# Fetching the first expert block before the routing is finished: a hybrid encoder step on one Trainium2 core

## The reference

```python
x = x + mix @ w_out                                   # the mixer, heads and pooling
h = rmsnorm(x, norm2_g)
pg_top, g = top_k(softmax(h @ w_rg + b_rg), 1)        # one of 4 groups
pv, pi = top_k(softmax((h @ w_re + b_re)[group g]), 2)  # two of its 4 experts
for e in range(16):                                   # D_MODEL 1024, D_EXPERT 512
    y = y + gates[:, e] * ((silu(h @ w_gate[e]) * (h @ w_up[e])) @ w_down[e])
out = rmsnorm(x + y, norm_f_g)
```

## Time and profile before

| what | value |
|---|---|
| median of 3 runs | 953.19 us (952.35 to 956.46) |
| profiled execution, its own time | 953.14 us |
| its span in the trace | 951.5 us |
| mixer stage, to the first instruction of block 1 | 547.29 us |
| blocks 1 to 15 | 547.29 to 904.15 us |
| last block's down product and the final norm | 904.15 to 951.5 us |

### The profile page before, as it was taken

The page is one execution under the profiler, slowest core; times in us unless marked ns, Lnnn a source line. Parts: engine busy times, 40 slices in busy tenths (PEclk is TensorE's granted clock), DMA queues, the critical chain, the costliest instruction groups (busy, mean ns, idle before and its releaser), DMA issues. The chain is left out here.

```text
span 951.5 us, 16708 instructions
## 1 busy us (share of the span) xinstructions
PE 885.8 (93%) x6335; PEld 753.2 (79%) x6335; DVE 435.8 (46%) x1169; ACT 145.6 (15%) x447; POOL 367.7 (39%) x572
## 2 busy tenths in 40 slices
PE   5989999999999999999986799999999999999960
PEld 3975969779596795968853399999999999999910
DVE  2245474737537365463656723434333333333254
ACT  2123122221312212121121000000000000000060
POOL 4050040300303012030120466777777777766512
PEclk9999999999999999999998799999999999999985
DMA  9931111030300202011065169999999999999874
GB/s 330 299 122 22 47 15 31 1 78 2 69 10 11 69 1 56 1 12 45 1 185 180 42 216 302 358 339 356 342 346 345 340 330 324 320 311 312 235 260 148
DMA packets 89973, 162.06 MB, mean 170 GB/s; under 512 B 48843, under 2 KB 58979, under 8 KB 81722
## 3 DMA queue, kind: packets, MB, share of 16 engines
q1 hardware_dynamic: 71210, 137.02, 41.2%
q0 software_dynamic: 17664, 24.23, 11.2%
q10 hardware_dynamic: 1040, 0.00, 0.1%
HBM read 138.78 MB, written 24.82 MB: 172 GB/s over the span
## 5 line engine op out<-in xcount | busy, mean ns | idle before, releaser
L1437 PE MATMUL bank<-wout,win 128*128 128x130 f32 (+3 forms) x2048 | 246.4, 282 | 3.1 <-DVE wout L1313 3.1
L1437 PEld LDWEIGHTS bank<-wout,win 128*128 128x128 f32 x2048 | 244.8, 191 | 3.2 <-DVE wout L1313 3.2
L1437 PE MATMUL bank<-hT,win 128*128 128x128 f32 (+1 forms) x1536 | 182.9, 279 | 0.0
L1437 PEld LDWEIGHTS bank<-hT,win 128*128 128x128 f32 x1536 | 178.6, 192 | 1.5 <-issue 1.2
L575 POOL DMA_INDIRECT z_d<-wout,win x75 | 119.3, 1590 | 27.9 <-issue 27.6
L1437 PE MATMUL bank<-win 128*128 128x130 f32 (+5 forms) x992 | 129.5, 290 | 0.0
L1437 PEld LDWEIGHTS bank<-win 128*128 128x128 f32 (+2 forms) x992 | 118.5, 188 | 8.9 <-issue 8.9
L1437 PE MATMUL bank<-win,hT 128*128 128x260 f32 (+3 forms) x512 | 119.7, 412 | 3.2 <-DMA win<-in_w_in 1.6
L1437 PE MATMUL bank<-wout,mixT 128*128 128x512 f32 (+1 forms) x384 | 118.5, 492 | 1.8 <-ACT mixT L815 1.7
L1437 PEld LDWEIGHTS bank<-win,hT 128*128 128x128 f32 (+1 forms) x512 | 76.1, 171 | 41.5 <-issue 32.5
L1437 PEld LDWEIGHTS bank<-wout,mixT 128*128 128x128 f32 (+1 forms) x384 | 51.4, 165 | 58.2 <-issue 55.5
(11 more groups left out here) (297 smaller groups left out, 821.4 us busy)
## 6 DMA issues: line engine op xcount, KB each, us to landing
win<-in_w_gate SPq DMA_DIRECT2D x32, 1024.0 KB, 6.2
win<-in_w_up SPq DMA_DIRECT2D x32, 1024.0 KB, 10.6
win<-in_w_down SPq DMA_DIRECT2D x32, 1024.0 KB, 9.6
win<-in_w_in SPq DMA_DIRECT2D x4, 2048.0 KB, 19.9
xbuf<-in_x_prompt SPq DMA_DIRECT2D x8, 512.0 KB, 3.9
wout<-in_w_out SPq DMA_DIRECT2D x1, 4096.0 KB, 15.2
z_d<-xbuf SPq DMA_DIRECT2D x32, 128.0 KB, 2.7
h_d<-xn SPq DMA_DIRECT2D x8, 512.0 KB, 2.8
```

What stands on the lines that cost most here:

```text
L1437: return nc.tensor.matmul(out, lhsT, rhs, start=first, stop=last)
```

## The change

The first block no longer waits for the complete list of expert 0. At i = LAST POOL writes the lists of the tiles up to 6, reads the first 150 entries of expert 0, and, after it has delivered the pooling mean, gathers those rows into a buffer of their own (`xg1`). An entry that is still empty brings row TOK, which now holds zeros (the plain store of a zero slice of `wr`). DVE turns and scales them (`first_turn`, `first_scale`) into `xgS` in the middle of the last tile's work. The rows of the last two tiles (`PICKED`, 7 and 8) are taken on PE instead: ACT copies the tile's rows from `xbuf` in another order (`xp`), DVE makes a matrix that holds the row's norm factor where the row's place in expert 0's list equals the column (`pick`), and `first_picks` on PE multiplies them, eight matmuls of 150 columns for each tile (16 instructions), added up in banks 2, 3 and 0. `first_rows` on DVE adds both parts into `xgT` in eight instructions.

Besides: expert 1 is fixed as well, as block 2 with 150 rows (so `SLOTS` has one more place of 150 and one fewer of 135); its list and its weights no longer wait for the table. `idraw` and `idt` have buffers of their own. The state's transposes on PE move ahead of `ranks(LAST)`. The copies and the stores of the state move from DVE and SP to ACT. POOL copies 256 rows of x_prompt into `h2_d` at i = 3, in place of values not yet written. `WARM` goes away. `first_turn` for block 1 and its five multiplies after the table go away, and `gather_turn(1)` comes after `products(1)`.

```diff
-    SLOTS = ((30, 1), (26, 6), (27, 3), (28, 2), (30, 2))
+    SLOTS = ((30, 1), (30, 1), (26, 6), (27, 2), (28, 2), (30, 2))
...
+        PICKED = (LAST - 1, LAST)
+        xp = [win[:, (15 + i) * D:(16 + i) * D].rearrange("p (k f) -> p k f", k=KD) for i in range(2)]
+        xg1 = win[:, 17 * D:17 * D + NP * PIECE].rearrange("p (a d) -> p a d", a=NP)
+        pick = [win[:, 19 * D + i * BLOCK:19 * D + (i + 1) * BLOCK].rearrange("p (a i) -> p a i", a=NP) for i in range(2)]
+        PICKB = ((2, 0, 3), (3, 3, 6), (0, 6, 8))
...
-        WARM = 14
...
-                sp.dma_start(rows[TOK, :].rearrange("(p n a) -> p n a", p=P, a=2), empty[:, 0:D // (2 * P), :]
-                             ).then_inc(S["ids_zeroed"], 16)
+                sp.dma_start(rows[TOK, :].rearrange("(p n) -> p n", p=P), wr[:, 0, NR:NR + D // P]).then_inc(S["ids_zeroed"], 16)
...
+                if t == PICKED[0]:
+                    after(sp, "h2_filled", 16)
...
-            after(sp, "table_ready", 1)
-            for c in range(NP):
-                sp.wait_ge(first[c], 16)
...
+            for half in range(2):
+                sp.wait_ge(*((gu_half, 2) if half == 0 else (gu_done, 8)))
+                load_gate_up(1, half)
+            for half in range(2):
+                sp.wait_ge(*((d0_used, 2) if half == 0 else (dn_done, 6)))
+                load_down(1, half)
+            after(sp, "table_ready", 1)
+            nblocks = sp.value_load(tabi[0:1, 2 * (NB + 1):2 * (NB + 1) + 1], min_val=NE, max_val=NB)
+            sooner = sp.value_load(tabi[0:1, 2 * (NB + 1) + 1:2 * (NB + 1) + 2], min_val=NE - 3, max_val=NB - 3)
+            with sp.Fori(3, nblocks + 1) as j:
...
+                if i == 3:
+                    early = [START[t] for t in PICKED]
+                    pool.dma_start(h2_d[min(early):max(early) + P, :], x_prompt[0, min(early):max(early) + P, :]
+                                   ).then_inc(S["h2_filled"], 16)
+                if i == LAST:
+                    scatter(i - 2)
+                    load_ids(0)
+                    pool.wait_ge(ids_in, 16)
+                    add_quarter(False)
...
+                    after(pool, "h2_stored", 16 * (LAST - 1))
+                    after(pool, "h2_filled", 16)
+                    after(pool, "u_done", NT)
+                    pool.wait_ge(carried, 1)
+                    gather_tokens(first, xg1)
+                elif 2 <= i:
...
             load_ids(0)
-            pool.wait_ge(ids_in, 16)
-            add_quarter()
+            pool.wait_ge(ids_in, 32)
+            g.tensor_copy(ents[0], idraw).then_inc(carried, 1)
             pool.wait_ge(carried, 2)
-            gather_tokens(first)
+            load_ids(CAP)
+            g.tensor_copy(ents[1], ents[0]).then_inc(rolled, 1)
+            pool.wait_ge(rolled, 1)
+            fetch_block(2, 2)
...
+                    a.activation(xp[t - PICKED[0]], xbuf[:, t % 4, :].rearrange("p (f k) -> p k f", k=KD), ACT.Copy
+                                 ).then_inc(xp_ready, 1)
...
+            after(act, "ulT_done", 1)
+            for n in range(2):
+                last = a.activation(uout[:, n, :], B[4 + n][0:HIST, :], ACT.Copy)
+            last.then_inc(S["ul_out"], 1)
+            after(act, "nT_done", 1)
+            a.activation(gt[:, :, :], B[6][0:H, 0:2 * P].rearrange("p (a b) -> p a b", a=2), ACT.Copy
+                         ).then_inc(S["nT_out"], 1)
+            after(act, "state_ready", NT)
+            for st, Co in ((Cp, C_prompt), (Cs, C_sample)):
+                act.dma_start(Co[0, 0].rearrange("h d v -> d h v"), st[:, :, 0:DH]).then_inc(S["stores"], 16)
...
+            def first_picks(t):
+                i, place = t - PICKED[0], rt[:, 80:81]
+                link(v.scalar_tensor_tensor(out=rt[:, 128 + i:129 + i], in0=oh[:, t, 2, 0:1], scalar=-NEAR, in1=place,
+                                            op0=ALU.mult, op1=ALU.add))
+                v.tensor_scalar(pick[i], place_of[:, :, :], rt[:, 128 + i:129 + i], sm[:, 11:12], ALU.is_equal, ALU.mult
+                                ).then_inc(pick_ready, 1)
+            def first_turn():
+                for c in range(NP):
+                    dve.wait_ge(first[c], 16)
+                    v.transpose(xgS[:, :, c, :], xg1[:, c, :].rearrange("p (i k) -> p k i", k=KD)).then_inc(xt_raw, 1)
+            def first_scale():
+                dve.wait_ge(xt_raw, NP)
+                v.tensor_tensor(xgS.rearrange("p k a i -> p k (a i)"), xgS.rearrange("p k a i -> p k (a i)"),
+                                wide(g2m[:, :], [P, KD, NP * 32]), ALU.mult).then_inc(base_scaled, 1)
+            def first_rows():
+                dve.wait_ge(base_scaled, 1)
+                after(dve, "out_done", NT)
+                for n, (b, k0, k1) in enumerate(PICKB):
+                    dve.wait_ge(picked, n + 1)
+                    for k in range(k0, k1):
+                        at = B[b][:, (k - k0) * BLOCK:(k - k0 + 1) * BLOCK].rearrange("p (a i) -> p a i", a=NP)
+                        v.scalar_tensor_tensor(out=xgT[:, k, :, 0:RP], in0=at, scalar=g2m[:, k:k + 1], in1=xgS[:, k, :, 0:RP],
+                                               op0=ALU.mult, op1=ALU.add).then_inc(gx_ready, 1)
...
                     h2_evac(LAST - 1)
+                    first_turn()
                     numerators(LAST)
                     partial_logits(LAST - 1)
                     head_out(LAST)
                     logits(LAST - 1)
                     routing(LAST - 1)
+                    first_scale()
                     residual(LAST)
...
+            first_rows()
...
-            def first_turn():
-                for c in range(NP):
-                    dve.wait_ge(first[c], 16)
-                    v.transpose(xgT[:, :, c, :], xg[:, c, :].rearrange("p (i k) -> p k i", k=KD)).then_inc(xt_raw, 1)
-                for c in range(NP):
-                    dve.wait_ge(xt_raw, c + 1)
-                    v.tensor_tensor(xgT[:, :, c, :], xgT[:, :, c, :], wide(g2m[:, :], [P, KD, 32]), ALU.mult).then_inc(gx_ready, 1)
...
+            products(1, SLOTS[0][0])
             gather_turn(1)
-            products(1, SLOTS[0][0])
...
+            def first_picks(t):
+                i = t - PICKED[0]
+                pe.wait_ge(xp_ready, i + 1)
+                pe.wait_ge(pick_ready, i + 1)
+                for b, k0, k1 in PICKB:
+                    for k in range(k0, k1):
+                        at = B[b][:, (k - k0) * BLOCK:(k - k0 + 1) * BLOCK].rearrange("p (a i) -> p a i", a=NP)
+                        last = mm(at, xp[i][:, k, :], pick[i], i == 0 and k == k0, i == 1 and k == k1 - 1)
+                    if i == 1:
+                        last.then_inc(picked, 1)
...
+                if i == NT + 1:
+                    first_picks(LAST - 1)
+                    state_transposes()
                 if 2 <= i:
                     ranks(i - 2)
+                if i == NT + 1:
+                    first_picks(LAST)
...
-            for _ in range(WARM):
-                mm(B[7][:, 0:512].rearrange("p (a b) -> p a b", a=4), ident[:, :],
-                   ident[:, :].unsqueeze(1).broadcast_to([P, 4, P]))
```

More of the change, by code:

```diff
@@ L562, in load_ids, with add_quarter @@
                                ).then_inc(ids_in, 16)
[L564 removed]
+            def add_quarter(keep=True):
                 g.tensor_scalar(idt, idraw[:, :, 0], qf[:, 0:1], None, ALU.add).then_inc(carried, 1)
[L567 removed]
+                if keep:
+                    g.tensor_copy(ents[0], idraw).then_inc(carried, 1)
+            after(pool, "hist_ready", 1)
+            after(pool, "ids_zeroed", 16 * 3)
+            for i in range(NT + 2):
+                if 1 <= i <= NT:
+                    causal(i - 1)
+                if i == 3:
[7 more added lines that the diff above has]
+                    add_quarter(False)
+                if i < NT:
+                    pool_mean(i)
+                if i == LAST:
+                    after(pool, "h2_stored", 16 * (LAST - 1))
[4 more added lines that the diff above has]
+                elif 2 <= i:
+                    scatter(i - 2)
             def stand(c):
@@ L1174, in _ @@
             link(v.tensor_scalar(ecap[:, :], iof[:, 0:NE], float(CAP), None, ALU.mult))
+            for a in range(NP):
+                v.tensor_scalar(place_of[:, a, :], iof[:, 0:RP], float(NP), a - NEAR, ALU.mult, ALU.add)
             p0 = 0
```

99 lines of the change are left out of this document (40 added, 59 removed).

## The result

The changed kernel takes **941.13 us** (median of 4 runs, 939.53 to 941.5), the kernel before, run beside it, 952.81 (4 runs). The ratio is 0.9868, 95% interval 0.9849 to 0.9887: faster by 1.3%. The forecast of 943.8 is a ratio of 943.8 / 953.19 = 0.9901, above that interval; the low end of the range, 940.5, is 0.9867. So sign and mechanism held, and the likeliest time was too slow by 2.7 us. The time fell where rival B stood (940.8, given a chance of 0.10); it also lies at the fast end of rival A's own range (941 to 946).

What follows compares the result with a forecast made beforehand. PE, busy 93% of the span, was taken to bound the kernel, with only block 1's start movable: start -11.8 us, larger block +2.4, so -9.4 and a forecast of 943.8 us, range 940.5 to 949.

Steps and rivals of the forecast that it cites:

- rival B: No clock dip and a quick clock: start 534.3, block 1 24.5, total 940.8 us; chance 0.10.
- rival A: The forecast as summed: 943.8 us, own range 941 to 946; chance 0.60.
- the routing: Expert stage: expert 1 gets 150 columns, still 16 blocks; one block costs 24.50 in place of 22.08 us, +2.4 us.
- POOL's early list: POOL before the last pooling mean: scatter, list load and offset take 8.0 of 10.0 idle us, costing nothing.
- the DVE part of the picks: Tile 7's pick matrix on DVE ahead of the last h2_evac: a scalar step and a compare, +0.45 us.
- the table's end: DVE's table, begun at 535.2, ends before 546.6; block 1's first silu product is due at 546.9: hidden by a hair.
- Block 2's rows: Gathered rows land at 552.2, are turned and scaled by 559.1 against a wanted 561.8: 2.7 us to spare.
- The copies on ACT: ACT's reordered copies into xp after each norm: 1.5 us taken, upper end 2.0, in 2.04 us idle; no cost.
- Block 1 itself: Block 1 on PE keeps its 26.3 us, clock dip included; ends 24.5 (no dip) and 28.
- step 6: PE between router sums and ranks: tile 7's picks and state transposes overfill the 4.75 us gap, +1.2 us (0.5 to 1.7).
- picks of tile 8: Sixteen PE instructions after the last places: 2.1 us at full clock to 4.1 at half, taken as 3.1.
- rival C: Clock stays low throughout: slower picks, block 1 28.0, output product loses 1.8 us; total 948.8 us; chance 0.15.

Runs made afterwards that it cites:

- The second run: The unchanged file of the changed kernel measured once more: 941.09 us, ratio 0.9858 against the kernel before.
- the one with the later turn: Changed kernel with first_turn moved on DVE behind routing(LAST-1) and first_scale put between the residual's halves: 940.65 us, ratio 0.9852.

## Why the prediction was right or wrong

**Right:** what bounds the kernel, and that block 1's start is the thing to move. PE's blocks have the lengths of the earlier trace rows, and the time follows the start. Also right, each by its row: the routing (16 blocks; +2.43 for +2.4, and +2.0 alone); POOL's early list (the pooling input finds POOL idle for 2.90 us at 470.97, forecast 2.0 to spare); the gathers, in before DVE's turn at 494.85, which waits for no DMA; `first_turn` at +1.33 for +1.6; the DVE part of the picks at +0.46 for +0.45; `first_scale` hidden; the table's end at 544.05 before the first silu product at 545.81. Block 2's rows are turned from 552.96 (forecast: landed at 552.2) and scaled by 556.99 against a wanted 558.75: 1.8 us to spare, forecast 2.7.

The copies on ACT took 2.04 us, at the forecast's upper end, not the 1.5 taken:

```profile
486.15 1.06 ACT L842 ACTIVATE xn<-xbuf 128x1024 f32<-128x1024 f32 x1 [3.98 <-DVE xbuf L1226]
...
487.77 2.04 ACT L845 ACTIVATE win<-xbuf 128x1024 f32<-128x1024 f32 x1
...
489.90 1.28 ACT L769 ACTIVATE dexp<-dexp,hmt 128x128 f32<-128x128 f32 x4
```

The same 1,024 columns take 1.06 us in order and 2.04 at a 32-byte step, and the decay matrix follows with no idle shown: the 2.04 us of the earlier trace rows were just enough. The Trainium skill ("SBUF — State Buffer", the note on cachelines) warns of this penalty without a price; the trace agrees and gives one, a factor of 1.9.

**Wrong, and the step that failed: "Block 1 itself ... I keep 26.3 us".** In the profiled execution, 941.5 us stand against a sum of 943.7. Block 1 measured 24.62, which is -1.7 us; its start is -1.4 us against the forecast; the kernel's end, +0.8, was not in the sum. The clock of 0.56 at block 1's start in the earlier trace rows was laid to no cause; it stood there after 3.15 us of idle, and the change leaves 1.15. The prediction named both gaps, left open whether the clock would be up, and kept the dip. The kernel before with 17 warm matmuls shows the cause: 0.58 us of idle, no dip. Rival B had both terms nearly right (start 534.3, block 1 24.5), with a chance of 0.10.

The second term of the same kind is PE in step 6 and the picks of tile 8. In the accounting of the last tile's chain:

| term, us | forecast | measured |
|---|---|---|
| slots of tile 6 later | 0 | +0.25 |
| `first_turn` | +1.6 | +1.33 |
| output product | 0 | +1.29 |
| `first_picks(7)` on DVE | +0.45 | +0.46 |
| PE up to the ranks | +1.2 | -0.4 |
| picks of tile 8 | 3.1 | 2.28 |

The first five add up to 2.9 us, as the ranks moved (528.66 - 525.75 = 2.91) where 3.25 were forecast; with the 0.8 of the picks that is nearly all of the 1.4 us by which block 1 starts earlier than the forecast 535.5.

Picks of tile 7 and transposes filled the gap of 4.75 us and no more. The picks did run at the low clock, 3.96 us for the 4.1 forecast:

```profile
524.00:527.00 3.00, 3.00 (x14) 3.00 (x14) 2.48 (x16) 0.00 (x0) 0.00 (x0) 0.50 0.44 175
```

Then the clock rose: the first eight transposes took 1.03 us in place of 1.87, the ranks 0.40 in place of 0.61, and the picks of tile 8 ran at full clock. So PE's part was a small gain where a loss was forecast. Both errors are one: the clock was carried over as a property of a place in time, not worked out from what PE does ahead of it. The mechanism of the sum was right, its sizes were not.

Against it stands the output product, a term that the main sum put at nothing and only rival C had: 10.12 us in this execution, 8.83 before the change, 7.13 at full clock. Windows in it, before and after:

```profile
508.00:510.00 2.00, 2.00 (x4) 0.85 (x3) 1.59 (x11) 0.39 (x3) 0.00 (x0) 0.55 0.03 12
```

```profile
510.00:513.00 3.00, 3.00 (x4) 1.01 (x3) 2.69 (x10) 0.39 (x3) 0.00 (x0) 0.50 0.00 0
```

Over the fourteen profiled executions of this document: where PE waited 1.66 us or more before the head transposes (five of them), the product took 8.74 to 10.12 us; where it waited 1.19 to 1.44 us, it took 7.13 in seven and 8.83 in two, the kernel before and the one with the later turn. So a longer wait and a slower product go together, but the wait alone doesn't decide, and that `first_turn` costs this much isn't shown. That the forecast came as near as 2.7 us is in part luck: this slower product and the later end, 2.1 us together, hid part of the miss. The second run's profiled execution, with a product of 8.83 us, took 939.49.

What the sum also missed, with no cost in either profile of the changed kernel: after it the loop of adds is no longer far from PE. In the kernel before, POOL was ready and waited 7.48 us for DVE's gate before the first adds of block 1:

```profile
575.98 0.18 POOL L492 TENSOR_TENSOR pad<-pad 1x1 f32<-1x1 f32 x1 [7.48 <-DVE wout L1356]
576.76 1.74 POOL L575 DMA_INDIRECT z_d<-wout,win  x1 [0.60 <-issue]
```

After the change PE starts 13.2 us earlier, but POOL's gathers only 4.5 (block 2's first at 542.97 against 547.46), and the adds come late:

```profile
565.10 1.56 DVE L1418 TENSOR_TENSOR wout<-wout,win 128x1280 f32<-128x1280 f32 x1 [5.64 <-POOL win L606]
...
568.25 1.73 POOL L595 DMA_INDIRECT z_d<-wout,win  x1 [0.58 <-issue]
```

Block 1's results ended at 559.5, but DVE's gate waits 5.64 us for POOL, which is still gathering block 3, and the first add is issued 8.8 us after the results; before the change that was 2.5 (574.3 to 576.8). As the loop's own period is about PE's 21.44 us, the lag is never made up while the blocks have 130 columns. The larger block 2 gives the loop 2.4 us of slack at the start. So the 2.4 us are paid, and yet taking them away alone gains nothing; with a second buffer it does.

The early start is not the only way into this lag. The kernel before with 17 warm matmuls starts block 1 later than the kernel before, and its page has the wait too:

```profile
L1349 DVE STREAM_TRANSPOSE wout<-bank 128x480 f32<-128x480 f32 (+1 forms) x45 | 26.2, 612 | 86.0 <-DMA z_d<-wout,win 35.0
```

There it begins with block 3, whose first add is issued 23.4 us after that of block 2. In the kernel before with the larger second place (58.7 us of such waits) it begins with block 7, 25.3 us after block 6. In neither does PE lose anything. So one late round of adds is enough to bring the loop close to PE, and the kernel before had little more room.

**Open:** why the output product takes 7.13, 8.83 or 10.12 us in executions of kernels that are the same up to there (10.12 and 8.83 of the changed file itself), and with it why the clock fell in it after gaps of 1.19 and 0.69 us in the kernel before, but not in block 1 after 1.15 us; how much of block 2's delay behind the table the weight loads make; and how the second place of 150 would do with two buffers, which wasn't tried.

## What to carry to other kernels

* Work out TensorE's clock from what it does ahead of the stretch, before and after the change: how long it idles, and whether the clock was up when the idle began. Useful matmuls in place of warm ones did as well here, and a gap of 1.15 us ahead of block 1 cost nothing where 3.15 cost 1.7 us. A short gap is no guarantee: the output product lost as much in the kernel before after gaps of 1.19 and 0.69 us. Where the rows leave it open, give the faster clock a chance to match.
* "The bound engine's stage is a fixed sum" holds while every loop beside it is shorter than its period. When you start the bound engine earlier, look up each such loop (results, adds, their landing, the buffer's next use). A loop as long as the period keeps its lag once it has one; then a saving elsewhere vanishes, and all that shows on the bound engine are gaps of a microsecond.
* A cost can hide behind a second limit: lift that one as well before you judge the first.

## What the runs showed of the hardware

* A small list load on POOL's queue: 2.18 us in a quiet stretch, 6.2 from issue to POOL's next step beside the weight loads; from the last gather's issue to DVE's turn 2.85 us in the kernel before, 4.8 in the changed one, 7.0 with the list behind the table.
* The granted clock after an idle stretch of TensorE, from 1.00 ahead of it: 0.50 after 3.74 us (and after 9.01), 0.56 after 3.15, 1.00 after 0.58 and after 1.15. But in the output product of the kernel before, 0.55 to 0.60 from 506 to 510 us after gaps of 1.19 and 0.69 us with 0.66 us of work between.
* ScalarE's copy of 1,024 columns at a 32-byte step takes 2.04 us against 1.06 in order.
* The landing of a block's last add into memory, beside weight loads, came 11.1 us after its issue (662.11 to 673.2); the five issues take 9.2 us in most blocks, up to 10.5.
